# Norm and rotation of branch B moved between the weight splits, row factors applied after the products, router on unscaled rows

## What is computed

```python
h = rms_norm(x, mix_pre_g[i])                 # y = x * rsqrt(mean(x*x) + eps) * g
z = h @ w_in[i]                               # columns for branches A, B, C, D and for the gates
q_b = axial_rope(rms_norm(q_b, b_q_g), ...)   # per head of 64
k_b = axial_rope(rms_norm(k_b, b_k_g), ...)
gates = sigmoid(z_gate)
x = x + rms_norm(mix, mix_post_g[i])
h = rms_norm(x, ffn_pre_g[i])
# layer 0: swiglu(h); layer 1: top 2 of 8 experts
logits = h @ w_router + b_router              # top-2, softmax, then SwiGLU of the chosen experts
x = x + rms_norm(f, ffn_post_g[i])
e = (p[i] @ ple_w_proj[i]) * sigmoid(x @ ple_w_gate[i])
x = x + rms_norm(e, ple_post_g[i])
```

## Time and profile before

| | |
|---|---|
| median of the runs | 1949.1 us (1948.28 to 1953.19) |
| profiled execution | 1947.06 us, span 1945.2 us |
| mean granted clock of PE | 0.985 |
| busy: PE, PE weight loads, DVE, ACT, POOL | 96%, 79%, 73%, 60%, 4% |
| PE waits for DVE's xn, over the kernel | 12.0 us in 2 waits |
| experts' part of the span | from about 935 to 1894 us |

### The profile page before, as it was taken

One profiled execution on the slowest core, in us unless ns is written; L12 is line 12 of the kernel. 1 busy time (PEld: TensorE's weight loads), 2 busy tenths in 40 slices (PEclk: granted clock), 3 DMA queues, 4 the chain that ended last, 5 costly groups with the idle time before them and its releaser, 6 DMA issues.

```text
span 1945.2 us, 26070 instructions
## 1 busy us (share of the span) xinstructions
PE 1866.2 (96%) x9632; PEld 1543.9 (79%) x9632; DVE 1412.8 (73%) x1453; ACT 1159.1 (60%) x1129; POOL 76.7 (4%) x130
## 2 busy tenths in 40 slices
PE   6899999999998899999999999999999999999996
PEld 5787677999996787677788888888888888888875
DVE  3568665555547557755689888888888888888875
ACT  4455553333335455554577777777777777777762
POOL 2101002000001000001000000000000000000010
PEclk9899999999999999999999999999999999999997
DMA  9547546555536633435799999999999999999990
GB/s 299 165 141 237 175 157 200 178 176 182 194 130 233 202 109 110 150 126 187 262 383 362 388 376 380 387 366 396 376 379 384 372 391 370 387 383 374 390 366 23
DMA packets 242816, 527.40 MB, mean 271 GB/s; under 512 B 9040, under 2 KB 58352, under 8 KB 242624
## 3 DMA queue, kind: packets, MB, share of 16 engines
q1 hardware_dynamic: 234272, 497.65, 71.5%
q0 software_dynamic: 6320, 21.02, 3.2%
q10 hardware_dynamic: 2160, 7.87, 1.0%
HBM read 510.78 MB, written 15.73 MB: 271 GB/s over the span
## 4 chain that ended last, share of the span: by engine, by line
PE 87%; DVE 4%; DMA 3%; ACT 2%; issue 2%; POOL 1%; SPq 1%; POOLq 0%; ACTq 0%; DVEq 0%
PE ps L1256 30%; PE ps L1199 19%; PE ps L1158 9%; PE ps L1055 9%; PE ps L1043 4%; PE ps L1382 4%; PE ps L1074 3%; PE ps L1021 2%; DMA ring<-in_w_in_dram 1%; PE ps L1228 1%; PE ps L1133 1%; PE ps L1426 1%; PE ps L1343 1%; DMA ring<-in_moe_w_down_dram 1%; PE ps L1412 1%
## 5 line engine op out<-in xcount | busy, mean ns | idle before, releaser
L2221 DVE TENSOR_TENSOR ring_lo<-ring,up_gate_hi_w 128x2048 fp32r<-128x2048 f32 x224 | 504.6, 2289 | 38.9 <-ACT up_gate_hi_w L1669 38.2
L1669 ACT CAST up_gate_hi_w<-ring 128x2048 fp32r<-128x2048 f32 x224 | 427.6, 1920 | 104.7 <-DMA ring<-in_moe_w_gate_dram 73.4
L1256 PE MATMUL ps<-up_gate_hi_w,tokens_hi 128*128 128x512 f32 x896 | 354.3, 395 | 2.3 <-DVE ring_lo L2221 1.5
L1256 PE MATMUL ps<-up_gate_hi_w,tokens_lo 128*128 128x512 f32 x896 | 349.6, 390 | 0.0
L1256 PE MATMUL ps<-ring_lo,tokens_hi 128*128 128x512 f32 x896 | 349.0, 389 | 0.0
L2226 DVE TENSOR_TENSOR down_lo_w<-ring,down_hi_w 128x2048 fp32r<-128x2048 f32 x112 | 255.8, 2284 | 0.3 <-ACT down_hi_w L1672 0.3
L1672 ACT CAST down_hi_w<-ring 128x2048 fp32r<-128x2048 f32 x112 | 214.1, 1919 | 67.5 <-DMA ring<-in_moe_w_down_dram 62.1
L1256 PEld LDWEIGHTS ps<-up_gate_hi_w,tokens_hi 128*128 128x128 f32 x896 | 168.3, 188 | 36.2 <-issue 1.9
L1256 PEld LDWEIGHTS ps<-up_gate_hi_w,tokens_lo 128*128 128x128 f32 x896 | 168.2, 188 | 35.8
L1256 PEld LDWEIGHTS ps<-ring_lo,tokens_hi 128*128 128x128 f32 x896 | 168.5, 188 | 33.5
L1199 PE MATMUL ps<-down_hi_w,hidden_hi 128*128 128x512 f32 x576 | 178.9, 392 | 1.9 <-DVE hidden_lo L2237 1.6
(11 more groups left out here) (268 smaller groups left out, 3041.5 us busy)
## 6 DMA issues: line engine op xcount, KB each, us to landing
ring<-in_moe_w_gate_dram SPq DMA_DIRECT2D x112, 1024.0 KB, 5.6
ring<-in_moe_w_up_dram SPq DMA_DIRECT2D x112, 1024.0 KB, 5.9
ring<-in_moe_w_down_dram SPq DMA_DIRECT2D x112, 1024.0 KB, 8.8
ring<-in_w_in_dram SPq DMA_DIRECT2D x58, 1024.0 KB, 5.3
ring<-in_ffn_w_up_dram SPq DMA_DIRECT2D x16, 1024.0 KB, 5.4
ring<-in_ffn_w_gate_dram SPq DMA_DIRECT2D x16, 1024.0 KB, 7.9
ring<-in_ffn_w_down_dram SPq DMA_DIRECT2D x16, 1024.0 KB, 9.6
expert_slot_rows<-work POOLq DMA_DIRECT2D x17, 512.0 KB, 4.9
```

The source lines that it names most:

```text
L1256: m = mm(bank, xs[:, 4 * half + k, :], w[:, k, :], start=(half == k == n == 0), stop=(half == 1 and k == 3 and n == 2))
L1669: copy(up_gate_hi_w[:, j, :], ring[:, slot, :]).then_inc(run.up_gate_hi, 1)
L2221: v.tensor_tensor(ring_lo[:, slot, :], ring[:, slot, :], up_gate_hi_w[:, j, :], ALU.subtract)\
```

## The change

- `MIXER` has `norm_b` after the first wide product, the squares of branch A (`square_a`) after the third, and the swap of B's q before the first narrow product. On DVE the squares of B stand after the splits for A0, its two multiplies per tile (`norm_b_scaled`) and the rotation of q's first tile in the splits for D0, that of the second tile in the splits for C0.
- `mixer_rows` writes x * gain, without the factor. The factor is applied where ACT copies a product to `z` (`z_out`), for narrow products in two copies instead of one, and as the scale of the gates' tanh (`half_rstd`, made by POOL).
- In layer 1 the first tile's turning for the mixer stands inside the PLE products (before the last of them), with `tile_his` and `tile_los` moved to match.
- Router: `router_rows` writes x * gain, logits get the factor at the copy (`logits_out`), `rows_normed` applies it to `xn` later. The first tile is turned before the last out product. The plain product for tile 0, second half, comes before the second logits, and its copy goes to a place of its own. The casts and splits of slots 2 and 3 move: slot 2's split after the choice of rows, slot 3's into the first chunk.
- At the start, SP waits for x of tile 0 after ring slot 0, and loads x of tile 1 after ring slot 1; ACT casts the turned tile 0 before the first weight.

```diff
-    steps = [("z", s) for s in WIDE_Z] + [("norm_b",), ("rope", "Bq"), ("rope", "Bk"), zn[0]]
-    steps += [("swap", "Bq"), ("swap", "Bk"), ("norm_a",), zn[1], ("swap", "An")]
+    steps = [("z", WIDE_Z[0]), ("norm_b",)] + [("z", s) for s in WIDE_Z[1:3]] + [("square_a",), ("z", WIDE_Z[3])]
+    steps += [("rope", "Bq"), ("swap", "Bq"), ("rope", "Bk"), zn[0], ("swap", "Bk"), ("norm_a",), zn[1], ("swap", "An")]
...
                     if pos == 0:
+                        sp.wait_ge(x_in_s[0], 32)
+                    if pos == 1:
                         for c in range(2):
                             sp.dma_start(x[64 * c:64 * c + 64, 1, :], x_v[c, 1]).then_inc(x_in_s[1], 16)
...
+            def halve(layer, t):
+
+                n = STAT[(layer, "pre", t)]
+                pool.wait_ge(rstd_done, n + 1)
+                nc.gpsimd.tensor_scalar(half_rstd[:, layer, t:t + 1], rstd[:, n:n + 1], 0.5, None, ALU.mult).then_inc(half_done, 1)
...
                         m = split_product(layer, "ple", i, t)
+                        if t == 1 and i == 2 and layer + 1 < DEPTH:
+                            turn_split_tile(layer + 1, "pre", xn, 0)
...
                         m = split_product(layer, "out", i, t)
                         if t == i == 0:
                             turn_merged(layer, 1, 1)
+                        if t == 1 and i == 2 and layer % 2:
+                            pe.wait_ge(scaled_done, 1)
+                            turn_tile(layer, "fpre", xn, 0)
...
-                        turn_tile(layer, "fpre", xn, t)
-                        emptied(layer, "fpre", t, 1)
                         if t == 0:
                             pe.wait_ge(params_in, PARAMS(layer))
+                        else:
+                            pe.wait_ge(scaled_done, t + 1)
+                            turn_tile(layer, "fpre", xn, t)
+                            plain_product(layer, 0, 1)
+                        emptied(layer, "fpre", t, 1)
...
-                activation(egate[:, t, :], ps[:, 6 + t, :], ACT.Tanh, scale=0.5).then_inc(egate_done, 1)
+                act.wait_ge(half_done, NT * (layer + 1))
+                activation(egate[:, t, :], ps[:, 6 + t, :], ACT.Tanh, scale=half_rstd[:, layer, t:t + 1]).then_inc(egate_done, 1)
+
+            def z_out(layer, t, c, w, bank):
+
+                k = STAT[(layer, "pre", t)]
+                act.wait_ge(rstd_done, k + 1)
+                return activation(z[:, t, c:c + w], bank, ACT.Copy, scale=rstd[:, k:k + 1])
...
-                            copy(z[:, :, c:c + w], bank.rearrange("p (t s) -> p t s", t=NT)).then_inc(ex_done, 1)
+                            for t in range(NT):
+                                ins = z_out(layer, t, c, w, bank[:, t * SEQ:t * SEQ + w])
+                            ins.then_inc(ex_done, 1)
...
+                def logits_out(t):
+
+                    bank = taken(layer, "logits", t)
+                    k = STAT[(layer, "fpre", t)]
+                    act.wait_ge(rstd_done, k + 1)
+                    activation(lg[:, t, :], bank[:, 0:8], ACT.Copy, scale=rstd[:, k:k + 1]).then_inc(ex_done, 1)
...
-                if layer % 2:
-                    for j in (2, 3):
-                        expert_his(main_pass, 0, j)
...
+                    activation(second_part, taken(layer, "proj", 0, 1), ACT.Copy, scale=0.5).then_inc(ex_done, 1)
+                    logits_out(1)
+                    expert_his(main_pass, 0, 2)
                     act.wait_ge(route_exp_in, 1)
                     activation(rt[:, 3, :], rt[:, 2, :], ACT.Exp).then_inc(route_exp, 1)
...
+            def router_rows(layer, t):
+
+                n = 5 * layer + 2
+                dve.wait_ge(gain_in[n % 2], 16 * (n // 2 + 1))
+                dve.wait_ge(x_done, X_COUNT(layer, 0, t))
+                v.tensor_tensor(xn[:, t, :], x[:, t, :], gain[:, n % 2, :], ALU.mult).then_inc(scaled_done, 1)
+
+            def rows_normed(layer, t):
+
+                k = STAT[(layer, "fpre", t)]
+                dve.wait_ge(rstd_done, k + 1)
+                dve.wait_ge(scaled_done, t + 1)
+                dve.wait_ge(ex_ready, USE[(layer, "fpre", t, 1)] + 1)
+                v.tensor_scalar(xn[:, t, :], xn[:, t, :], rstd[:, k:k + 1], None, ALU.mult).then_inc(xn_done, 1)
+
+            def mixer_rows(layer, t):
+
+
+                n = 5 * layer
+                dve.wait_ge(gain_in[n % 2], 16 * (n // 2 + 1))
+                if layer:
+                    dve.wait_ge(x_done, X_COUNT(layer - 1, 2, t))
+                v.tensor_tensor(xn[:, t, :], x[:, t, :], gain[:, n % 2, :], ALU.mult).then_inc(xn_done, 1)
...
+                        i = WIDE_Z.index(s[1])
+                        z_los(layer, i + 1, 0)
+                        if i == 1:
+                            norm_b_scaled(layer)
+                        elif i == 2:
+                            rope(layer, "Bq", tiles=(1,))
+                        z_los(layer, i + 1, 1)
+                        if i == 1:
+                            rope(layer, "Bq", tiles=(0,))
...
-                    expert_los(main_pass, 0, 2)
+                    for t in range(NT):
+                        rows_normed(layer, t)
                     route()
                     expert_pass(main_pass)
```

More of the change, by code:

```diff
@@ L252, in exchange_uses @@
                     add(layer, "fpre", t, b)
+                if t:
+                    add(layer, "proj", 0, 1)
                 add(layer, "logits", t)
@@ L256, in exchange_uses @@
                     add(layer, "proj", 0, 0)
+            rest = (1, 0), (1, 1)
         else:
             add(layer, "pt")
-            add(layer, "proj", 0, 0)
-        for t, half in ((0, 1), (1, 0), (1, 1)):
+            rest = (0, 0), (0, 1), (1, 0), (1, 1)
+        for t, half in rest:
             add(layer, "proj", t, half)
@@ L464, in trunk @@
         minus_half = sb("minus_half", [P, NT * 6])
+        half_rstd = sb("half_rstd", [P, DEPTH, NT])
         peak = sb("peak", [P, 2, NT, 2])
@@ L922, in _ @@
                 stat(0, "pre", t)
+                halve(0, t)
             load_gain(1)
@@ L960, in _ @@
                     pool.wait_ge(rows_known, 1)
+                    pool.wait_ge(xn_done, 2 * NT * (layer + 1))
                     for t in range(NT):
@@ L986, in _ @@
                         stat(layer + 1, "pre", t)
+                        halve(layer + 1, t)
                 load_gain(5 * layer + 6)
@@ L1489, in _ @@
                 else:
-                    for t, half in ((0, 1), (1, 0), (1, 1)):
-                        plain_product(layer, t, half)
+                    for half in range(2):
+                        plain_product(layer, 1, half)
                     pe.wait_ge(routed, 1)
@@ L1802, in _ @@
                                 bank = taken(layer, "z", c, t)
-                                copy(z[:, t, c:c + w], bank[:, 0:w]).then_inc(ex_done, 1)
+                                z_out(layer, t, c, w, bank[:, 0:w]).then_inc(ex_done, 1)
                         else:
@@ L1909, in _ @@
                 else:
-                    copy(lg[:, NT - 1, :], taken(layer, "logits", NT - 1)[:, 0:8]).then_inc(ex_done, 1)
-                    plain_part(layer, halved, 0, 1)
+                    activation(second_part, taken(layer, "proj", 0, 1), ACT.Copy, scale=0.5).then_inc(ex_done, 1)
+                    logits_out(1)
+                    expert_his(main_pass, 0, 2)
                     act.wait_ge(route_exp_in, 1)
@@ L2082, in stage, with rope @@
                 return staged[:, n % 2]
-            def rope(layer, item):
+            def rope(layer, item, tiles=range(NT)):
                 if layer == 0 and item == "Bq":
@@ L2116, in rope @@
                         dve.wait_ge(ex_done, Z_DONE[(layer, D0)] + 1)
-                for t in range(NT):
+                for t in tiles:
                     src = z[:, t, col:col + heads * HD].rearrange("p (h d) -> p h d", h=heads)
@@ L2138, in rope @@
                         link(last)
-                last.then_inc(staged_done, 1)
+                if NT - 1 in tiles:
+                    last.then_inc(staged_done, 1)
             def softmax(layer, j, b, h):
@@ L2330, in ple_ends @@
                     dve.wait_ge(ple_prod, n + 1)
-                    if t == 1 and layer + 1 < DEPTH:
-                        tile_los(layer + 1, "pre", 0)
                     residual(layer, "ple", 4, t, e, ple_tmp[:, t, :])
                     if layer + 1 < DEPTH:
-                        normed(layer + 1, "pre", 0, t)
+                        mixer_rows(layer + 1, t)
+                        if t == 0:
+                            tile_los(layer + 1, "pre", 0)
             def expert_chunk(run):
@@ L2367, in expert_pass @@
                     check_overflow()
+                    expert_los(run, 0, 2)
                 for_chunks(dve, expert_chunk(run))
@@ L2412, in _ @@
                     if s[0] == "z" and s[1] in WIDE_Z[:-1]:
-                        for half in range(2):
```

(8 more changed lines are left out.)

54 lines of the change are left out of this document (31 added, 23 removed).

## The result

The kernel after took 1937.19 us (median; 1935.93 to 1938.59) against 1950.67 us (1948.28 to 1953.19) for the kernel before beside it: a ratio of 0.9933, 95% interval 0.992 to 0.9946. The profiled execution took 1937.19 us for a span of 1935.2, 9.9 us less than the profiled one of before. So it is faster by 0.7%, but 6.7 us above the forecast and just above the range.

What follows compares the result with a forecast made beforehand. PE, busy in 96% of the span, bounds the kernel; only four short places where it waits can move. Terms sum to -18.4 us: 1947.1 to 1928.7 profiled, plus 2.0 for the median, rounded to 1930.5 us, range 1922 to 1937.

Steps and rivals of the forecast that it cites:

- The prediction's own sign of being wrong: Mixer's wide products: a halved clock there was listed among the signs that would show the forecast wrong; no size.
- The head of the mixer: Both layers, branch B's norm in the split gaps: PE's waits and the halved clock go, -8.3 us and -7.2 us.
- The start of layer 0: Before D0: squares of B wait for all parameters ahead of D0's first split, +2.0 us, bounds 0 and +5.
- POOL held by DVE: Layer 0: POOL's power starts only after D0's first split, delaying scaling and second split, +1.5 us, bounds 0 and +2.5.
- PE's wait before D0's second half: Layer 0's head: a PE wait of about 1.5 us there was listed as a sign of being right.
- Between the layers: Layer 0 to 1: tile 0 turned before the last PLE product, rows without factor, -2.2 us, bounds -3 and -0.5.
- The copies: Fourteen narrow copies become two scaled ones each, eight ahead of copies PE waits for: +0.8 us, bounds 0 and +2.
- The router: Out products' end to first expert product: earlier turn, splits behind the choice of rows, -5.0 us, bounds -7.5 and -1.5.
- the router gives it back: Router rival: halvings fall on two plain products and the gathering, -1.5 instead of -5.0 us, 1934.2 us; chance 0.14.
- The one of short gaps: Mixer's head rival: DVE pieces hold the splits, clock drops once per layer in wide products, +10 us, 1940.7; chance 0.08.

Runs made afterwards that it cites:

- Experiment 9: Mixer's head as before the change (norm B, its rotations and norm A behind all wide products), rest as the kernel after: 1945.26 us, ratio 0.9979 to the kernel before.
- Experiment 1: Kernel after with DVE's wait for the parameters' transfer moved behind the squares of norm B: 1931.0 us, ratio 0.9892 to the kernel before.
- experiment 5: Kernel after with ACT's copy of plain product (1,0) moved ahead of its wait for the router's exponential: 1935.33 us, ratio 0.9917 to the kernel before.

## Why the prediction was wrong

Two steps failed. The sum priced the waits that PE keeps or gets by their length alone, and the half clock behind three of them cost 6.6 us more (2.7 in D0 and C0, 2.5 between the layers, 1.4 at chunk 1). And the chain through the router gave 2.3 us where it was put at 5.0. The prediction's own sign of being wrong, a halved clock in the wide products, came true in D0 and in tile 1's first product. The 2.0 us added for the median above the profiled run came to nothing (1937.19 us both), so the forecast's miss of 6.7 hides 8.5 by the traces.

**The head of the mixer: right.** From C0's end to the third narrow product PE takes 13.4 us where it took 22.2 (-8.9 against -8.3), and layer 1's head gives -7.8 against -7.2; waits and clock went as said from C0's end on. Experiment 9, which puts the old head back, shows that the gain is the head's.

**The start of layer 0: right in kind, too small, and one step missing.** D0 starts 3.34 us late, not 2.0. Prediction and trace name the same wait; the last parameter landed at 40.21 and not at 38.2, since x's second tile landed at 16.10 (14.39 before) and POOL's issues waited for its square. The missing step is the clock: the late start was priced by its length alone, and the wait of 4.75 us in front of a wide product cost 2.7 more. Experiment 1 shows both.

**POOL held by DVE: the mechanism is there, its price is not.** The power started only at the split's end and the scaling waited 2.49 us, as worked out (+1.5), but PE did not wait for the second split. D0's first half, 5.6 us at full clock, would have ended at 50.6 us and the split ended at 51.98; at half clock the product lasted past it. In experiment 1, where DVE waits 1.93 us between squares and split, the power (36.56 to 38.87) began before the split and nothing was held. PE's wait before D0's second half, announced as 1.5, is in neither.

**Between the layers: -2.2, exactly, and then 2.5 given back by the clock.** The step that failed is the reading of the earlier trace rows: two waits before wide products had left the clock at full, and I took that for any two waits. The change put them side by side.

**The copies: mis-sized.** 1.9 us instead of 0.8. The row of 0.39 us for 256 columns, without a factor per row, stood in for the scaled copy, which took 0.47.

**The router: -2.3 instead of -5.0** (-3.4 from the out products' end to chunk 1's start, less the 1.0 of the turn that moved ahead of that end). The chain from the out products' end to the gathering took 18.9 us where the working gives 16.6 (928.9 less 912.3): a copy behind the exponential (1.4, experiment 5) and a plain product at half clock (3.09 for 2.0). The rest was lost where the prediction did not look. It ended the stage at chunk 0's first product, which came 5.0 us closer to the out products' end (28.8 before, 23.8 now), 4.0 net of the moved turn. But the scatter had moved close to chunk 1's loads, they took 6.9 and 8.1 us for 5.2, and chunk 1 waits for a load that leaves only when chunk 0 has read its slot.

**The rivals.** That the router gives it back was near in amount (-1.5, and -2.3 found), but the gathering, which it put at half clock, ran at full. The one of short gaps with one halving in the wide products of each layer (1940.7) came about as near to the measured time as the one above (1934.2), by luck: the halvings came from the parameters' wait and from the early turn, not from DVE's pieces in the gaps. I had given it 0.08, and read the clock as a thing of the old head. Stage by stage the 8.5 us between the sum of -18.4 and the -9.9 found are: the clock in D0 and C0 +2.7, between the layers +2.5, at chunk 1 +1.4; the router's copy, half clock and loads +2.7; the bodies of both layers +1.2 (the copies 1.1 of it); the start -0.2 (1.3 later than said, POOL's 1.5 not paid); the heads -1.2; and the end, -0.7.

## What to carry to other kernels

Each wait that a change leaves or makes on the matrix engine has to be priced twice, for its length and for the clock behind it, and two short waits with little between them cost it here (1.76 and 1.56 us around a turn of 1.1), where a longer pair around a full product did not. In the seven executions that had them, the half clock cost 1.3 to 2.9 us. A wait belongs in front of the first instruction that reads what it waits for: moving a block of work moves every wait that stood at its head. When a stage is brought forward, look past its end for the next transfer that it now runs into.

## What the runs showed of the hardware

- Two executions of one kernel had the half clock in the router at different places (907 and 941 us; 907 and 920), while those at 43 and 627 us repeated. A change worth under 3 us there could only be read by stages.
- Chunk 1's first product ran at half clock in the four executions where PE had waited 2.86 to 3.16 us ahead of it (4.42 to 4.58 us), and at full in the nine where it had waited 1.19 to 2.11 (2.97 to 3.01).
- The two 1 MB gate loads of chunk 1 took 5.0 to 5.2 us where the scatter's last issue had ended 1.56 us or more ahead, though its rows were still landing for up to 1.7 us, and 5.7 to 8.1 where they left before or at that end.
- POOL's scaling of B's squares took 2.16 us beside a DVE split of 2.28 and 0.19 without one (experiment 1).
- A scaled copy of 128x512 from PSUM took 0.69 us against 0.59 for the plain one.
